# Twenty-four column tiles of the first projections as twelve pairs of seven block products, the short tile first

## What is computed

```python
u = rmsnorm(x, norm_mix[l])
proj = u @ w_in[l]        # q, k (4 + 4 tiles of 128 columns), v, r (8 + 8), 32 columns of low rank,
...                       # then 20 more tiles: pooling input and the gates
q, k, v, r, lr = ...      # gated linear attention in four heads, from these columns
...
x = x + merged @ w_out[l]
x = x + (silu(gate) * up) @ w_ffn_out[l]
```

## Time and profile before

| | |
|---|---|
| median of 3 runs | 2748.24 us (2747.73 to 2749.09) |
| the profiled execution | 2749.12 us, of which the span between first and last instruction is 2747.3 us |
| PE busy | 96% of the span, 12530 matmul records |
| DVE, ACT, POOL busy | 63%, 36%, 46% |
| DMA | 340.30 MB, mean 124 GB/s |
| the first projections | from 25.6 us (first matmul of unit 0) to 309.8 us (`z`) |

### The profile page before, as it was taken

The page is one execution under the profiler, slowest core; times in us unless marked ns, Lnnn a source line. Parts: engine busy times, 40 slices in busy tenths (PEclk is TensorE's granted clock), DMA queues, the critical chain, the costliest instruction groups (busy, mean ns, idle before and its releaser), DMA issues.

```text
span 2747.3 us, 32550 instructions
## 1 busy us (share of the span) xinstructions
PE 2642.3 (96%) x12530; PEld 2131.1 (78%) x12530; DVE 1733.2 (63%) x1925; ACT 983.3 (36%) x1354; POOL 1266.4 (46%) x767
## 2 busy tenths in 40 slices
PE   7999999999999999999999899989898999999998
PEld 5888788787778788888777688756786888877777
DVE  4111355565747766667889656666548766777887
ACT  4000333343223333334335211657445333434444
POOL 2343323223445888886333353241034988823331
PEclk9999999999999999999999999999999999999999
DMA  5223333324442333336633352401323545654543
GB/s 185 92 99 102 106 101 114 122 91 155 138 146 77 89 115 115 100 109 201 201 112 106 113 167 90 140 1 45 108 77 108 154 141 168 200 165 153 169 138 138
DMA packets 332499, 340.30 MB, mean 124 GB/s; under 512 B 18315, under 2 KB 254454, under 8 KB 332358
## 3 DMA queue, kind: packets, MB, share of 16 engines
q1 hardware_dynamic: 322790, 302.73, 35.5%
q10 hardware_dynamic: 9568, 35.66, 3.3%
HBM read 229.01 MB, written 108.30 MB: 123 GB/s over the span
## 4 chain that ended last, share of the span: by engine, by line
PE 51%; DVE 9%; issue 2%; DMA 2%; ACT 2%; POOL 1%; SPq 0%; DVEq 0%; ACTq 0%; POOLq 0%
PE ps L3288 35%; PE ps L531 8%; PE ps L2361 2%; DVE op_lo L3365 2%; PE ps L2384 1%; PE ps L2371 1%; DVE sw_lo L3198 1%; DMA op_raw<-hidden 1%; DVE acc L3609 1%; PE ps L2864 0%; DVE acc L1887 0%; DVE x L2308 0%; DVE acc L3616 0%; DMA x_block<-acc 0%; DVE op_lo L3268 0%
## 5 line engine op out<-in xcount | busy, mean ns | idle before, releaser
L3288 PE MATMUL ps<-op_hi,sw_hi 128*128 128x512 f32 x1769 | 693.5, 392 | 17.2 <-DVE op_lo L3365 9.9
L3288 PE MATMUL ps<-op_hi,sw_lo 128*128 128x512 f32 x1769 | 690.5, 390 | 0.0
L3288 PE MATMUL ps<-op_lo,sw_hi 128*128 128x512 f32 x1769 | 690.3, 390 | 0.0
L497 POOL TENSOR_TENSOR w_hi_t<-w_raw,ones 128x1024 fp32r<-128x1024 f32 (+1 forms) x85 | 163.5, 1926 | 714.5 <-PE ps L531 344.5
L3288 PEld LDWEIGHTS ps<-op_hi,sw_hi 128*128 128x128 f32 x1769 | 333.3, 188 | 98.0 <-issue 18.2
L3288 PEld LDWEIGHTS ps<-op_hi,sw_lo 128*128 128x128 f32 x1769 | 333.3, 188 | 70.0
L3288 PEld LDWEIGHTS ps<-op_lo,sw_hi 128*128 128x128 f32 x1769 | 333.2, 188 | 68.9 <-issue 0.5
L654 DVE TENSOR_TENSOR stage<-ps,rstd 128x1024 f32<-128x1024 f32 x62 | 75.8, 1222 | 355.3 <-PE ps L531 336.9
L3188 ACT ACTIVATE sw_hi<-sw_sumNone 128x512 fp32r<-128x512 f32 (+1 forms) x252 | 157.1, 624 | 333.8 <-PE ps L3288 252.5
L531 PE MATMUL ps<-h1hi,w_hi_t 128*128 128x512 f32 x720 | 229.6, 400 | 13.0 <-DVE h1lo L615 9.0
L3198 POOL TENSOR_TENSOR sw_lo<-sw_sumNone,sw_hi 128x512 fp32r<-128x512 f32 x138 | 213.5, 1557 | 34.4 <-ACT sw_hi L3188 34.3
(11 more groups left out here) (434 smaller groups left out, 4636.2 us busy)
## 6 DMA issues: line engine op xcount, KB each, us to landing
op_raw<-hidden SPq DMA_DIRECT2D x42, 1024.0 KB, 8.7
w_raw<-in_w_in SPq DMA_DIRECT2D x60, 512.0 KB, 4.0
sw_raw<-in_w_ffn_in SPq DMA_DIRECT2D x44, 512.0 KB, 5.4
proj<-stage ACTq DMA_DIRECT2D x42, 512.0 KB, 2.6
hidden<-hidden_blocks SPq DMA_DIRECT2D x13, 1536.0 KB, 6.1
hidden<-hidden_blocks SPq DMA_DIRECT2D x14, 1280.0 KB, 5.0
sw_raw<-in_w_up SPq DMA_DIRECT2D x32, 512.0 KB, 8.3
sw_raw<-in_w_down SPq DMA_DIRECT2D x32, 512.0 KB, 5.2
```

The lines of the kernel that those rows point to most:

```text
L497: ins = pool.tensor_tensor(whi[:, u.par, s], raw[:, u.par, s], ones[:, 0:1].to_broadcast([P, n]), ALU.mult)
L3288: mm = pe.matmul(out, w, x[:, k, :], start=(k == 0 and i == 0 and r < 4), stop=(k == n - 1 and i == 2), skip_group_check=r >= 4)
```

## The change

The low-rank tile is now unit 0. Its result is scaled straight into `lrT`. The 24 other tiles become twelve pairs. A pair takes the weights of its two tiles as four blocks (two tiles by two halves of the 1024 features) and the activations as four blocks (two halves of the features by two halves of the tokens), and makes the two output tiles with seven block products r = 0 to 6 instead of eight. Each has 4 k-steps by 3 terms, 12 matmuls of 512 columns. Four of the seven weight operands are sums that POOL makes (`in_sum`); ACT makes the high parts (`in_hi`), DVE the low ones (`in_lo`; POOL those of the third and fourth). Four of the activation operands, T1 to T4, are sums and differences of the blocks of h1: DVE makes them (`t1_dve`, `t2_dve`, `t34_dve`), ACT and DVE split them (`t_hi`, `t_lo`, 2048 elements a partition). After the products DVE adds up what belongs together and scales by `rstd` (`in_post`): nine instructions of 512 elements a pair. SP stores four pieces of 256 KB a pair.

Pairs 0 and 1 take turns product by product in the order 0, 4, 3, 1, 2, 5, 6; the other ten are done one by one in the order 0 to 6. Even pairs load into `raw`, odd ones into `stage`. Sums and results lie in `acc`, so that they wait for the spill of x, and q, k, v, r and the helpers of the attention have other rows of `acc` than before. The 20 later units are numbered from 1 on, and POOL splits the first two of them behind the last block products.

The diff, with one level of indentation taken off; names of tiles, semaphore counts and later stages' counts are left out:

```diff
-N_IN = 45
+N_IN = 21
+N_PROJ = 45
...
+IN_PAIRS = [t for h in range(GH) for t in ((h, 4 + h), (8 + 2 * h, 9 + 2 * h), (16 + 2 * h, 17 + 2 * h))]
...
+IN_ORDER = (0, 1, 2, 3, 4, 5, 6)
+IN_FIRST = (0, 4, 3, 1, 2, 5, 6)
+IN_SEQ = [(p, r) for r in IN_FIRST for p in range(2)] + [(p, r) for p in range(2, N_INP) for r in IN_ORDER]
...
+def in_posts(p, r):
+    if p < 2:
+return {1: ("u2",), 2: ("u3", "22", "22s", "11"), 5: ("21", "21s"), 6: ("12", "12s")}.get(r, ())
+    return {1: ("u2",), 2: ("u3",), 3: ("22", "22s"), 4: ("11",), 5: ("21", "21s"), 6: ("12", "12s")}.get(r, ())
...
+IN_SUM_OF = {3: 1, 1: 2, 2: 3, 6: 4}
...
+def in_pair_load(sp, p):
+    if p == 0:
+        sp.wait_ge(S["w_split"], 1)
+    if p >= 2:
+        sp.wait_ge(S["in_lo"], IN_AT[p - 2, 6] + 1)
+    for i, c in enumerate(IN_PAIRS[p]):
+        sp.dma_start(in_raw[p % 2][:, i, :, :], w_in[:, :, c * P:(c + 1) * P]).then_inc(S["w_landed"][p % 2], 16)
+def in_store(sp, p, what):
+    sp.wait_ge(S["in_post"], IN_POST[p, what if what == "11" else what + "s"])
+    i, j = int(what[0]) - 1, int(what[1]) - 1
+    c = IN_PAIRS[p][i]
+    sp.dma_start(proj[c * P:(c + 1) * P, j * HALF:(j + 1) * HALF], in_out[p % 2][what])\
+      .then_inc(S["stored"][p % 2], 16)
 def in_sp(sp):
...
+    load_unit(sp, Step(U_IN), w_in[:, :, LR0:LR0 + P])
+    in_pair_load(sp, 1)
+    in_pair_load(sp, 0)
+    for p in range(N_INP):
+        if p + 2 < N_INP:
+            in_pair_load(sp, p + 2)
+        in_store(sp, p, "22")
+        if p == IN_LAST:
+            sp.wait_ge(S["in_lo"], N_IN_SEQ)
+            sp.dma_start(gv, tile_of(proj, 8, 2)).then_inc(S["v_loaded"], 16)
+        in_store(sp, p, "11")
+        if p == IN_LAST - 1:
+            sp.wait_ge(S["in_lo"], IN_AT[p, 6] + 1)
+            sp.wait_ge(*in_landed(IN_LAST))
+            for u in (MID0, MID0 + 1):
+                mid_weights(sp, u)
+        in_store(sp, p, "21")
+        in_store(sp, p, "12")
+        if p == IN_LAST - 1:
+            sp.wait_ge(S["stored"][0], IN_STORED)
+            sp.dma_start(gq, proj[0:P, :]).then_inc(S["qk_loaded"], 16)
+            sp.dma_start(gk, proj[4 * P:5 * P, :]).then_inc(S["qk_loaded"], 16)
+def in_sum(pool, p, which):
+    a11, a12, a21, a22 = in_blocks(p)
+    s1, s2, s3 = in_sums_of(p)
+    if which == 1:
+        pool.wait_ge(*in_landed(p))
+        if p >= 2:
+            pool.wait_ge(S["in_lo"], IN_AT[p - 1 if p > 2 else 0, 3] + 1)
+        pool.tensor_tensor(s1, a21, a22, ALU.add).then_inc(S["in_sum"], 1)
+    elif which == 2:
+        pool.wait_ge(S["in_sum"], IN_SUM[p, 1])
+        if p == 1:
+            pool.wait_ge(S["t_fresh"], 2)
+        if p >= 2:
+            pool.wait_ge(S["in_lo"], IN_AT[p - 1 if p > 2 else 0, 6] + 1)
+        pool.tensor_tensor(s2, s1, a11, ALU.subtract).then_inc(S["in_sum"], 1)
+    elif which == 3:
+        if p == 0:
+            pool.wait_ge(S["t_fresh"], 2)
+        if p >= 2:
+            pool.wait_ge(S["in_lo"], IN_AT[p - 1 if p > 2 else 0, 2] + 1)
+        pool.tensor_tensor(s3, a21, a11, ALU.subtract).then_inc(S["in_sum"], 1)
+    else:
+        pool.wait_ge(S["in_sum"], IN_SUM[p, 2])
+        pool.wait_ge(S["in_lo"], IN_AT[p, 1] + 1)
+        pool.tensor_tensor(s2, a12, s2, ALU.subtract).then_inc(S["in_sum"], 1)
+def in_hi(act, m):
+    p, r = IN_SEQ[m]
+    act.wait_ge(*in_landed(p))
+    if r in IN_SUM_OF:
+        act.wait_ge(S["in_sum"], IN_SUM[p, IN_SUM_OF[r]])
+    if m >= 4:
+        act.wait_ge(S["in_product"], m - 3)
+    elif m >= 2:
+        act.wait_ge(S["unit_done"], U_IN + 1)
+    act.activation(in_ring(whi, m), in_block(p, r), ACT.Copy).then_inc(S["in_hi"], 1)
+POOL_LOW = (2, 3)
...
+def in_lo(eng, m):
+    eng.wait_ge(S["in_hi"], m + 1)
+    if m and (m in POOL_LOW) != (m - 1 in POOL_LOW):
+        eng.wait_ge(S["in_lo"], m)
+    eng.tensor_tensor(in_ring(wlo, m), in_block(*IN_SEQ[m]), in_ring(whi, m).bitcast(F32), ALU.subtract)\
+       .then_inc(S["in_lo"], 1)
 def in_pool(pool):
...
+    split_unit(pool, Step(U_IN))
+    for m in POOL_LOW:
+        in_lo(pool, m)
+    pool.wait_ge(S["x_spilled"], 16)
+    pool.wait_ge(S["t_fresh"], 1)
+    for which in (1, 2, 3, 4):
+        for p in range(2):
+            in_sum(pool, p, which)
+    for p in range(2, N_INP):
+        for which in (1, 3, 2, 4):
+            in_sum(pool, p, which)
+def in_product(pe, m):
+    p, r = IN_SEQ[m]
+    if r == 0 and p >= 2:
+        pe.wait_ge(S["in_post"], IN_POST[p - 2, "12"])
+    if r == 4:
+        pe.wait_ge(S["in_first"], p + 1)
+    if r == 5:
+        pe.wait_ge(S["in_post"], IN_POST[p, "u3"])
+    if r == 6:
+        pe.wait_ge(S["in_post"], IN_POST[p, "22"])
+    if (p, r) == (0, 1):
+        pe.wait_ge(S["rstd_ready"], NORM_AT["mix"] + 1)
+    if (p, r) == (1, 1):
+        pe.wait_ge(S["unit_out"][0], 1)
+    pe.wait_ge(S["in_lo"], m + 1)
+    if r in T_OF:
+        pe.wait_ge(S["lo_ready"], KT + T_OF[r] + 1)
+        hi, lo = thi[T_OF[r]], tlo[T_OF[r]]
+    else:
+        pe.wait_ge(S["lo_ready"], KT)
+        hi, lo = [part(t, *{0: (0, 0), 4: (1, 0), 6: (1, 1)}[r]) for t in (h1hi, h1lo)]
+    out = in_bank(p, r)
+    opens = r in ((0, 1, 2, 3))
+    for k in range(4):
+        wh, wl = in_ring(whi, m)[:, k * P:(k + 1) * P], in_ring(wlo, m)[:, k * P:(k + 1) * P]
+        for i, (w, x) in enumerate(((wh, hi), (wh, lo), (wl, hi))):
+            mm = pe.matmul(out, w, x[:, k, :], start=(opens and k == 0 and i == 0), stop=(k == 3 and i == 2),
+                           skip_group_check=not opens)
+    mm.then_inc(S["in_product"], 1)
...
 def in_pe(pe):
...
+    mm_unit(pe, Step(U_IN), h1hi, h1lo, to=PS[3], wait_k=lo_wait(pe, "mix"))
+    norm_sum(pe, "mix", KT, ps=1)
+    for m in range(N_IN_SEQ):
+        if m == 3:
+            norm_spread(pe, "mix", ps=1)
+        in_product(pe, m)
+def in_first(act, p):
+    act.wait_ge(S["in_product"], IN_AT[p, 0] + 1)
+    if p < 2:
+        act.wait_ge(S["t_fresh"], p + 1)
+        act.wait_ge(S["x_spilled"], 16)
+    else:
+        act.wait_ge(S["in_post"], IN_POST[p - 2, "u2"])
+    act.activation(in_firsts[p % 2], in_bank(p, 0), ACT.Copy).then_inc(S["in_first"], 1)
+def t_hi(act, i):
+    if i == 0:
+        act.wait_ge(S["t_gained"], 1)
+    else:
+        act.wait_ge(S["t_fresh"], i + 1)
+    act.activation(thi[i][:, :, :], (t1, t2, t3, t4)[i][:, :, :], ACT.Copy).then_inc(S["hi_ready"], 1)
+def t1_gained(act):
+    act.wait_ge(S["t_fresh"], 1)
+    for k in range(4):
+        ins = act.activation(t1[:, k, :], t1[:, k, :], ACT.Copy, scale=col("norm_mix", k))
+    ins.then_inc(S["t_gained"], 1)
 def in_act(act):
...
+    for m in range(4):
+        in_hi(act, m)
+    in_first(act, 0)
+    t1_gained(act)
+    in_first(act, 1)
+    t_hi(act, 0)
+    in_hi(act, 4)
+    in_hi(act, 5)
+    norm_root(act, "mix", rstd[:, :], ps=1)
+    t_hi(act, 1)
+    in_hi(act, 6)
+    in_hi(act, 7)
+    t_hi(act, 2)
+    in_hi(act, 8)
+    in_hi(act, 9)
+    t_hi(act, 3)
+    for m in range(6, N_IN_SEQ):
+        p, r = IN_SEQ[m]
+        if r == 0:
+            in_first(act, p)
+        if m + 4 < N_IN_SEQ:
+            in_hi(act, m + 4)
+def t1_dve(dve):
+    dve.tensor_tensor(t1[:, :, :], part(acc, 0, 1), part(acc, 0, 0), ALU.subtract).then_inc(S["t_fresh"], 1)
+def t2_dve(dve):
+    dve.wait_ge(S["t_gained"], 1)
+    for k in range(4):
+        ins = dve.scalar_tensor_tensor(out=t2[:, k, :], in0=part(acc, 1, 1)[:, k, :],
+                                       scalar=col("norm_mix", 4 + k), in1=t1[:, k, :],
...
+def t34_dve(dve, i):
...
+    for k in range(4):
+        ins = dve.scalar_tensor_tensor(out=(t3, t4)[i][:, k, :], in0=part(acc, i, 0)[:, k, :],
+                                       scalar=col("norm_mix", 4 * i + k), in1=t2[:, k, :],
...
+def t_lo(dve, i):
+    dve.wait_ge(S["hi_ready"], KT + i + 1)
+    dve.wait_ge(S["t_fresh"], max(2, i + 1))
+    dve.tensor_tensor(tlo[i][:, :, :], (t1, t2, t3, t4)[i][:, :, :], thi[i][:, :, :].bitcast(F32),
+                      ALU.subtract).then_inc(S["lo_ready"], 1)
+def lr_dve(dve):
+    dve.wait_ge(S["unit_done"], U_IN + 1)
+    dve.wait_ge(S["rstd_ready"], NORM_AT["mix"] + 1)
+    dve.tensor_tensor(lrT, PS[3][0:32, :], rstd[0:32, :], ALU.mult).then_inc(S["unit_out"][0], 1)
+def in_post(dve, p, what):
+    r = {"u2": 1, "u3": 2, "22": 3, "11": 4, "21": 5, "12": 6}.get(what)
+    if r is None:
+        t, j = in_out[p % 2][what[:2]], int(what[1]) - 1
+        dve.wait_ge(S["in_post"], IN_POST[p, what[:2]])
+        ins = dve.tensor_tensor(t, t, rstd[:, j * HALF:(j + 1) * HALF], ALU.mult)
+    else:
+        dve.wait_ge(S["in_product"], IN_AT[p, r] + 1)
+        if what in IN_OUTS and p >= 2:
+            dve.wait_ge(S["stored"][p % 2], 64 * (p // 2))
+        if what == "u2":
+            dve.wait_ge(S["in_first"], p + 1)
+            ins = dve.tensor_tensor(in_u2[p % 2], in_bank(p, 1), in_firsts[p % 2], ALU.add)
+        elif what == "11":
+            ins = dve.tensor_tensor(in_out[p % 2]["11"], in_bank(p, 4), rstd[:, 0:HALF], ALU.mult)
+        else:
```

(33 more changed lines are left out.)

164 lines of the change are left out of this document (97 added, 67 removed).

## The result

The changed kernel takes 2722.39 us (median of 4 runs, 2720.94 to 2724.12), the kernel before, measured beside it, 2747.98 us (2747.19 to 2749.09). The ratio is 0.9907, with a 95% interval of 0.989 to 0.9924. It is faster, by 25.6 us; the forecast was 16.8. Measured again beside a second set of runs of the kernel before, the ratio is 0.9907 too. The profiled run took 2720.94 us, its span is 2719.2 us.

What follows compares the result with a forecast made beforehand. The prediction took the stage to be bound by TensorE's matmul count. Its terms, -32.6 - 3.0 + 11.9 + 3.7 + 3.2, summed to -16.8 us, from a median of 2748.24 to 2731.4 us, range 2719 to 2742.

Steps and rivals of the forecast that it cites:

- the main term: First projections, twelve pairs: 144 fewer matmuls on TensorE at 0.2262 us each, -32.6 us.
- Rivals 2 and 3: Pairs: ties between them lose the gain (2741 to 2751 us, chance 0.08), or VectorE binds ten pairs (2759, 0.06).
- The opening: Until block (0,5) may start: VectorE's queue, lengthened by GpSimd, keeps TensorE waiting, +11.9 us.
- Ten meetings of 1.05 us: Opening: each of ten GpSimd instructions meets VectorE on SBUF and costs VectorE 1.05 us, up to 10.5 us.
- ScalarE in the opening: Opening, up to block (0,5): the sum counted VectorE's work and GpSimd's meetings, with no wait for ScalarE.
- VectorE's own work, 32 us: Opening, up to the end of `u3`: VectorE's listed instructions take 32 us without GpSimd's meetings.
- The first step, -3.0: Short tile, before the block products: GpSimd's second split goes, the first step takes 2.4 us instead of 5.5, -3.0 us.
- Pair 2, +3.7: Block (2,0): addition `12` is queued behind a low part that needs pair 2's load, so TensorE waits, +3.7 us.
- The clock, +3.2: After two waits TensorE runs at the lower clock for eight matmul intervals, 1.6 us each time, +3.2 us.
- TensorE's idle time, some 15 us between 43 and 101: Sign from the opening to pair 2: TensorE idle some 15 us; forecast wrong if the opening's idle is under 8 or over 22.
- Nothing gained behind z.: Stage's end and later stages: nothing gained or lost; forecast wrong if the span after `z` changes by over 2 us.
- Rival 1: Opening mostly covered, ScalarE's high parts keeping VectorE and GpSimd apart: wait some 2 us, in all -28.3, 2720 us; chance 0.12.

Runs made afterwards that it cites:

- second profile: The changed kernel, unaltered, measured and profiled once more; 2724.00 us.
- last variant: Changed kernel with three queue orders altered and pair 0's additions moved forward, then three low parts put ahead of VectorE's third T sum; 2719.30 us.
- low-behind variant: Changed kernel with the sixteenth block's low part put behind pair 0's twelfth addition in VectorE's queue; 2720.68 us.

## Why the prediction was right, and where not

The sign and the main term were right, and their grounds were shown: TensorE alone binds the stage, at 0.226 us a matmul (120 added: 27.4 us). The time of 2722.39 us lies near the lower end of the range, 2719 to 2742. The Trainium skill's 216 ns (TensorE: Matmul & The Clock Gate, "Back-to-back issue gap") was rightly set aside; no stretch here shows it. Rivals 2 and 3 did not come: from 110 us on TensorE has no gap. The size was off by 8.8 us, 3.9 of it in the stage and 4.9 behind `z`. The opening itself came out near, 10.3 against 11.9, but by luck: `u3` was done at 81.6 against 84.1 since VectorE began 0.9 us earlier, had 1.5 us less work of its own, paid 6.5 less for meetings and waited 6.4 for ScalarE. The steps:

- **Ten meetings of 1.05 us.** This is the step that failed. Meetings cost VectorE 4.0 us, not 10.5: the price of one was about right, the count was not. Some of GpSimd's instructions ran while VectorE waited for ScalarE, GpSimd itself waited for T2 and for low parts, and in the longest meeting it was GpSimd that stood still. The Trainium skill's lock for the whole instruction (SBUF — State Buffer, "Who interferes with whom") agrees in kind with GpSimd's 7.68 us; the rows say besides who paid, and that it stood still through several of VectorE's instructions, not one.
- **ScalarE in the opening.** It was costed at nothing. It holds VectorE for 6.4 us. Of these, 2.5 are there because the copy of block (1,0) stands ahead of the first high part in ScalarE's queue and waits for T2; with the order changed they turn into meetings. Another 2.48 are the scaling of T1, which is made at 44.2 but scaled from 46.4 on, behind the copy of block (0,0), which waits for TensorE; no run moves that one.
- **VectorE's own work, 32 us.** It was 30.5. The forecast took 2.5 us for each of five instructions of 2048, the mean of a group; here one without company has the next start 2.2 us behind it.
- **The first step, -3.0.** It gave -3.8. The forecast put the first copy into the sum of squares at the 1.21 us of an addition; without company the copy takes 0.69.
- **Pair 2, +3.7.** The mechanism was right, link by link: landing 90.1 (93.3), block (2,0) 96.88 (100.2). The wait was 2.7 since this chain ran 3.3 us ahead of the forecast, and TensorE, done with its four blocks at 94.0 (96.5), only 2.5.
- **The clock, +3.2.** It was 3.4, for the two waits that the forecast named. It held the slow stretch inside the opening to be free, and the rows agree: block (0,5) was released by VectorE's `u3`, and VectorE had idled only for ScalarE. In the second profile the same two waits are followed by 3.4 and by nothing.
- **TensorE's idle time, some 15 us between 43 and 101.** It was 10.0: of the opening's 10.3 us of lateness 7.3 were idle, the rest mostly slow matmuls.
- **"Nothing gained behind z."** The forecast named a change by over 2 us as proof against it. 2.5 us go with the load of `hidden`; the rest of the 5 us between the medians is of the size of the spread of these runs.

Rival 1 gave 2720 and is nearer in its time, and its reason, that ScalarE would keep VectorE and GpSimd apart, is what the run with the high part ahead shows; but its opening with 2 us of waiting was not there, 7.3 was. The 5 us behind `z`, for which it had nothing either, brought it near.

## What to carry to other kernels

A stage that one engine binds without gaps gives back every instruction that is taken from it; the cost of a new algorithm is in its first few units, before the rings between the engines are full, and is read there instruction by instruction, ScalarE's included. There, look for a ready instruction that stands behind one that waits for a load: one such order was worth 2.5 to 3.5 us here, while the wait at block (0,3) only moved when its releaser was brought forward, because two engines then met that had been apart. A meeting of VectorE and GpSimd has a steady price, some 1.0 us here, but not every GpSimd instruction is one that VectorE pays for: ask which of the two is held by something else at that moment.

## What was not expected

- A GpSimd instruction of 128 x 512 that takes 1.29 us alone took 7.68 us beside a run of VectorE's low parts and sums without idle time, while these kept their own times. At 56.35 us in the last variant VectorE pays: two low parts took 3.48 us in place of 1.27. What decides which of them stands still is not shown.
- Waits of 0.91 to 1.42 us left TensorE's clock at 1.00 in each place looked at; after waits of 2.1 to 3.1 us the clock was most often at the lower level for a stretch, but not each time: the wait of 2.81 us at block (0,3) in the low-behind variant, those of 2.54 and 2.58 at block (2,0) with the high part ahead and with ScalarE's stores, and that of 2.12 at block (0,5) without the first sums lie in or before windows of 10 us at 1.00.
- Programs that are alike from some point on differ there by up to 6.6 us in profiled runs. A gain under that is read from a stage's marks, not from one span.
